# Attention projections of a hybrid backbone block: neighbouring channels exchanged by two transfers per head instead of a matrix product

## The chip, the cores and the metric

The kernel runs on one NeuronCore of a Trainium2 chip. The metric is the device time of one execution in microseconds (us). A core has five instruction queues that work side by side and meet only at semaphores: TensorE (PE in the rows; its weight loads are PEld), VectorE (DVE), ScalarE (ACT), GpSimd (POOL) and SyncE (SP), which issues the DMA transfers here.

## The reference

Two layers over 256 context tokens and 512 latent tokens of width 1024: an RWKV-7 layer, then a grouped-query attention layer, each followed by a SwiGLU feed-forward. The change is in the attention layer's projections. Cut to what matters:

```python
q = rms_norm((h @ wq).reshape(B, n, 8, 128), gq)      # 8 query heads
k = rms_norm((h @ wk).reshape(B, n, 2, 128), gk)      # 2 key heads
v = (h @ wv).reshape(B, n, 2, 128)
# rotation, latent tokens only, over pairs of neighbouring channels
x1, x2 = x[..., 0::2], x[..., 1::2]
out = stack([x1 * cos - x2 * sin, x1 * sin + x2 * cos])
```

Channels lie on the 128 partitions, tokens along the free axis. So `x * cos + partner(x) * sin` is wanted, where `partner` exchanges the partitions 2i and 2i+1, and the table `sin` carries the sign.

## The kernel before

The function `qkv` (lines 3001 on) makes v for all tokens, then ten heads one after the other: heads 0 and 1 are keys (768 tokens), heads 2 to 9 queries (512 latent tokens). Each engine runs a list of steps n = 0 to 11, and three heads are in work at once in a step:

- **Weights.** SP loads head n's weights, 512 KB, into one of two buffers `qk_w_raw` (`w.load`, L531). ACT rounds them (`w.round`, L536), POOL makes the remainder (`w.subtract`, L541). SP waits before load n only for the remainder of head n-2, which frees the buffer (L3058 to L3060).
- **PE, step n.** The product of head n: 24 matmuls with 512 columns (L561, called at L3084; for key heads 24 more with 256). Then the sum of squares of head n-1 by a product with ones (L3093). Then, for head n-2, the exchange of neighbouring channels: a product of the head in `qk_raw` with a permutation `swap` into bank 4 (L3103, two calls for two halves of the partitions, four instructions each in fp32 as the trace counts them for both together). It waits for `normed`.
- **ACT, step n.** First round the weights of head n+1 (L3125), then the square root for head n-1 (L3130), then copy head n from its bank to `qk_raw` (L3138) and square it (L3141). The copy of head n waits until head n-2 is `rotated`, since both use the same `qk_raw` buffer.
- **DVE, step n.** For head n-2: multiply by cos (L3168), wait for `swapped`, multiply the exchanged channels by sin (L3177), add (L3178, signals `rotated`). Then for head n-1: the reciprocal of the root (L3183), and the scaling (L3185), which signals `normed`.

Every engine's list is in program order, so an instruction whose semaphore is late holds all behind it on its engine. When all ten heads are done, a barrier ends the block and `attend` begins (it issues its own weight loads and starts with the scores).

Of the kernel before, what the change touches and what calls it, by code (L numbers as in the profile page):

```python
# [21 lines left out]
ALU = mybir.AluOpType  # L22
# [3 lines left out]
P = 128  # L26
D = 1024
CT = D // P
CTX, LAT = 256, 512
TOK = CTX + LAT  # L30
# [15 lines left out]
HEADS, KV_HEADS = 8, 2  # L46
# [35 lines left out]
def signal(eng, ins, sem, value):  # L82

    ins.then_inc(sem, 1)
    eng.wait_ge(sem, value)


def need(eng, sem, n):

    if not isinstance(n, int) or n > 0:  # L90
        eng.wait_ge(sem, n)
# [11 lines left out]
def half(h):  # L103

    return slice(CH * h, CH * h + CH)


class Core:
# [5 lines left out]
    def sb(self, name, shape):  # L114
        return self.ctx.enter_context(self.nc.sbuf_tensor(name, shape, F32))

    def sem(self, name):
        return self.ctx.enter_context(self.nc.semaphore(name))
# [439 lines left out]
def three_passes(pe, out, w, x, first, last, onto=False):  # L558

    for n, (a, b) in enumerate(((w[0], x[0]), (w[0], x[1]), (w[1], x[0]))):  # L560
        mm = pe.matmul(out, a, b, start=(first and n == 0), stop=(last and n == 2), skip_group_check=onto)  # L561
    return mm
# [2438 lines left out]
def qkv(c, d, h, hi, lo, q, k, v, norm):  # L3001
# [6 lines left out]
    NH = KV_HEADS + HEADS  # L3008
    KVD = KV_HEADS * P
    with ExitStack() as ctx:  # L3010
        sb = lambda n, s: ctx.enter_context(nc.sbuf_tensor(n, s, F32))
        sem = lambda n: ctx.enter_context(nc.semaphore(n))
        w = SplitWeights(c, ctx, "qk_w", CT, NH, (NH // 2, NH // 2))
        V_BANKS = (0, 1, 2, 3, 6, 7)
        wv = sb("wv", [P, CT, KVD])
        wv_hi, wv_lo = (ctx.enter_context(nc.sbuf_tensor(n, [P, CT, KVD], F32R)) for n in ("wv_hi", "wv_lo"))
        cos, sin, swap = sb("cos", [P, LAT]), sb("sin", [P, LAT]), sb("swap", [P, P])
        raw = [sb(f"qk_raw{s}", [P, TOK]) for s in range(2)]
        sq = [sb(f"qk_sq{s}", [P, TOK]) for s in range(2)]
        std, turned = sb("qk_std", [P, TOK]), sb("qk_turned", [P, LAT])  # L3020
# [1 line left out]
        tables, v_loaded, v_rounded = sem("rope_loaded"), sem("wv_loaded"), sem("wv_rounded")  # L3022
        v_rest = [sem(f"wv_rest{n}") for n in range(2)]
        v_product, v_copied = sem("v_product"), sem("v_copied")
        copied, squared, summed, rooted, normed, swapped, rotated, order_sem = (sem(n) for n in (
            "qk_copied", "qk_squared", "qk_summed", "qk_rooted", "qk_normed", "qk_swapped", "qk_rotated", "qk_dve_order"))
        wk = d["at_wk"][0].rearrange("(k p) e -> p k e", p=P)
        wq = d["at_wq"][0].rearrange("(k p) e -> p k e", p=P)

        def segs_of(n):  # L3030
            return SEGS if isinstance(n, int) and n < KV_HEADS else SEGS[1:]

        def steps(eng, step, order=None):

            for n in range(4):
                step(n, n % 2)
            for n in range(4, NH - 2):
                step(n, n % 2)
            for n in range(NH - 2, NH + 2):
                step(n, n % 2)  # L3040
# [5 lines left out]
        def there(n):  # L3046

            return not isinstance(n, int) or 0 <= n < NH

        with nc.Block() as block:  # L3050
            @block.sync
            def _(sp):
                sp.dma_start(wv[:], d["at_wv"][0].rearrange("(k p) e -> p k e", p=P)).then_inc(v_loaded, 16)
                for s in range(2):
                    w.load(sp, s, s, wk[:, :, s * P:(s + 1) * P])
                for t, s in ((cos, "k_cos"), (sin, "k_sin"), (swap, "k_swap")):
                    sp.dma_start(t[:], d[s]).then_inc(tables, 16)
                with sp.Fori(0, HEADS // 2) as i:  # L3058
                    for s in range(2):
                        w.load(sp, 2 * i + s + KV_HEADS, s, wq[:, :, bass.ds((2 * i + s) * P, P)])  # L3060

            @block.tensor
            def _(pe):
                norm.sums(pe)
                norm.spread(pe)
                for kt in range(CT):
                    norm.ready(pe, kt)
                    if kt % (CT // 2) == 0:
                        pe.wait_ge(v_rest[kt // (CT // 2)], 1)
                    for t in range(TOK // P):  # L3070
                        at = slice(t * P, t * P + P)
                        mm = three_passes(pe, c.bank[V_BANKS[t]][:, 0:KVD], (hi[:, kt, at], lo[:, kt, at]),
                                          (wv_hi[:, kt, :], wv_lo[:, kt, :]), kt == 0, kt == CT - 1)
                        if kt == CT - 1:
                            mm.then_inc(v_product, 1)
                pe.wait_ge(v_copied, TOK // P)

                def step(n, s, i=None):
                    if there(n):
                        pe.wait_ge(w.rest, w.at + n + 1)  # L3080
                        need(pe, copied, n - 1)
                        for kt in range(CT):
                            for at, width in segs_of(n):
                                mm = three_passes(pe, c.bank[2 * s + (at > 0)][:, 0:width], (w.hi[s][:, kt, :], w.lo[s][:, kt, :]),  # L3084
                                                  (hi[:, kt, at:at + width], lo[:, kt, at:at + width]),
                                                  kt == 0, kt == CT - 1)
                        mm.then_inc(w.product, 1)
                    if there(n - 1):

                        pe.wait_ge(squared, n)  # L3090
                        need(pe, rooted, n - 1)
                        for at, width in segs_of(n - 1):
                            mm = pe.matmul(c.bank[5 + (at > 0)][:, 0:width], c.ones[:], sq[1 - s][:, at:at + width],  # L3093
                                           start=True, stop=True)
                        mm.then_inc(summed, 1)
                    if there(n - 2):

                        if isinstance(n, int) and n == KV_HEADS:
                            pe.wait_ge(tables, 48)
                        pe.wait_ge(normed, n - 1)  # L3100
                        need(pe, rotated, n - 2)
                        for b in range(2):
                            mm = pe.matmul(c.bank[4][half(b), 0:LAT], swap[half(b), half(b)], raw[s][half(b), CTX:TOK],  # L3103
                                           start=True, stop=True)
                        mm.then_inc(swapped, 1)

                steps(pe, step)

            @block.scalar
# [49 lines left out]
            @block.vector  # L3159
            def _(dve):  # L3160
                order = Order(dve, order_sem)
                v_ = nc.vector

                def step(n, s, i=None):
                    if there(n - 2):
                        head = n - 2
                        x = raw[s]
                        order(v_.tensor_tensor(turned[:], x[:, CTX:TOK], cos[:], ALU.mult))  # L3168
                        dve.wait_ge(swapped, n - 1)
                        if isinstance(n, int) and head < KV_HEADS:  # L3170
                            o = k[:, head, CTX:TOK]
                            order(v_.tensor_copy(k[:, head, 0:CTX], x[:, 0:CTX]))
                        else:
                            at = head - KV_HEADS
                            at = slice(at, at + 1) if isinstance(n, int) else bass.ds(at, 1)
                            o = q[:, at, :].rearrange("p o t -> p (o t)")
                        order(v_.tensor_tensor(o, c.bank[4][:, 0:LAT], sin[:], ALU.mult))  # L3177
                        signal(dve, v_.tensor_tensor(o, o, turned[:], ALU.add), rotated, n - 1)  # L3178
                    if there(n - 1):
                        at = segs_of(n - 1)[0][0]  # L3180
                        gain = PGK if at == 0 else PGQ
                        dve.wait_ge(rooted, n)
                        order(v_.reciprocal(std[:, at:], std[:, at:]))  # L3183
                        x = raw[1 - s]
                        signal(dve, v_.scalar_tensor_tensor(x[:, at:], x[:, at:], c.par[:, gain:gain + 1], std[:, at:],  # L3185
                                                            ALU.mult, ALU.mult), normed, n)

                norm.invert(dve)
                norm.scale(dve, 0)
                norm.scale(dve, 1)  # L3190
                for k_tile in range(CT):
                    if k_tile + 2 < CT:
                        norm.scale(dve, k_tile + 2)
                    norm.low(dve, k_tile)
                steps(dve, step, order)


# [284 lines left out]
```

## Time and profile before

| | |
|---|---|
| median of 3 runs | 2188.77 us (2188.66 to 2190.41) |
| profiled execution, span | 2190.7 us |
| attention projections with their norm and v | about 1497 to 1632.5 us of that span |
| the ten heads, from the first scaling's start to the last sum's end | 1556.3 to 1632.4 us |
| PE busy over the span | 92% |
| DVE, ACT, POOL busy | 55%, 38%, 17% |

The span is what the profiler saw from the first to the last instruction of one execution; it is 1.9 us over the median of the runs. Times in rows are counted from the start of that span.

### The profile page before, as it was taken

To read this page: it belongs to the slowest core of one execution; us is meant where nothing else is said; L and a number is where in the kernel's file an instruction comes from. 1 tells how busy PE (TensorE), PEld (TensorE's weight loads), DVE (VectorE), ACT (ScalarE), POOL (GpSimd) and SP (SyncE) were. 2 spreads that over 40 slices of the span, in tenths; PEclk is the share of its full clock that TensorE was granted. 3 is DMA by queue.
4 is the path that set the end of the run, shared out by engine and by line. 5 is a ranking of instruction groups with operands and counts; after the bars stand their busy time and mean duration, and the time that the engine had idled before them with its cause. 6 is when DMAs were issued, how large, how long until landed. Compare 5 with 4: busy or idle time off the path is not lost. (4 is left out here: it accounts for less than half of the span.)

```text
span 2190.7 us, 52634 instructions
## 1 busy us (share of the span) xinstructions
PE 2022.6 (92%) x22455; PEld 1755.4 (80%) x22455; DVE 1209.5 (55%) x1909; ACT 830.5 (38%) x1395; POOL 365.9 (17%) x387
## 2 busy tenths in 40 slices
PE   5799997899999988689999999998979988999998
PEld 3688885688888887689999999998645577888887
DVE  4865435566666663328857667565675534333333
ACT  2433324455555533226324233234325424422321
POOL 0000001566666652020000000002210010000000
PEclk8799998799999999789999999998989998999999
DMA  9577774001111000511212122112110013332332
GB/s 317 178 238 228 230 239 140 19 19 30 34 35 36 18 12 11 180 59 40 94 58 77 59 80 75 58 58 59 58 29 1 1 58 96 96 112 81 97 112 78
DMA packets 223496, 191.70 MB, mean 88 GB/s; under 512 B 12970, under 2 KB 208180, under 8 KB 222772
## 3 DMA queue, kind: packets, MB, share of 16 engines
q1 hardware_dynamic: 223284, 188.58, 27.8%
q8 instruction: 169, 2.77, 0.5%
q14 instruction: 43, 0.35, 0.1%
HBM read 170.73 MB, written 17.83 MB: 86 GB/s over the span
## 5 line engine op out<-in xcount | busy, mean ns | idle before, releaser
L541 DVE TENSOR_TENSOR ffn_lo<-ffn_raw,ffn_hi 128x1024 fp32r<-128x1024 f32 (+1 forms) x58 | 77.5, 1335 | 196.5 <-ACT ffn_hi L536 196.5
L561 PE MATMUL banks<-operand_hi,ffn_w_hi 128*128 128x384 f32 x464 | 155.9, 336 | 4.4 <-DVE operand_lo L507 4.4
L561 PE MATMUL banks<-operand_lo,ffn_w_hi 128*128 128x384 f32 x464 | 155.6, 335 | 0.0
L561 PE MATMUL banks<-operand_hi,ffn_w_lo 128*128 128x384 f32 x464 | 155.5, 335 | 0.0
L561 PE MATMUL banks<-mix_hi,proj_hi 128*128 128x386 f32 (+1 forms) x384 | 136.6, 356 | 14.8 <-DVE proj_lo L733 9.5
L561 PE MATMUL banks<-operand_hi,ffn_hi 128*128 128x512 f32 x352 | 138.6, 394 | 5.2 <-DVE operand_lo L507 2.8
L561 PE MATMUL banks<-operand_hi,ffn_lo 128*128 128x512 f32 x352 | 138.1, 392 | 0.0
L561 PE MATMUL banks<-operand_lo,ffn_hi 128*128 128x512 f32 x352 | 138.1, 392 | 0.0
L536 ACT CAST ffn_hi<-ffn_raw 128x1024 fp32r<-128x1024 f32 (+1 forms) x60 | 68.3, 1139 | 183.2 <-PE banks L561 182.4
L561 PE MATMUL banks<-mix_hi,proj_lo 128*128 128x386 f32 (+1 forms) x384 | 131.8, 343 | 0.0
L561 PE MATMUL banks<-mix_lo,proj_hi 128*128 128x386 f32 (+1 forms) x384 | 131.8, 343 | 0.0
L431 POOL TENSOR_TENSOR norm_squares<-norm_squares,norm_x 128x768 f32<-128x768 f32 (+1 forms) x18 | 29.8, 1654 | 588.3 <-ACT norm_x L425 588.3
L2827 ACT CAST ffn_w_hi<-ffn_raw 128x512 fp32r<-128x512 f32 (+1 forms) x116 | 68.7, 605 | 130.2 <-PE banks L561 130.1
L2060 POOL TENSOR_TENSOR lvl<-sc_b,level_mask 128x256 f32<-128x256 f32 x144 | 109.6, 777 | 48.1 <-DVE sc_b L1792 34.2
L561 PE MATMUL banks<-ffn_t_hi,ffn_w_hi 128*128 128x384 f32 x320 | 106.9, 334 | 0.0
L561 PE MATMUL banks<-ffn_t_lo,ffn_w_hi 128*128 128x384 f32 x320 | 106.9, 334 | 0.0
L561 PE MATMUL banks<-ffn_t_hi,ffn_w_lo 128*128 128x384 f32 x320 | 106.9, 334 | 0.0
L2994 DVE SCALAR_TENSOR_TENSOR residual_stream<-banks,mod,residual_stream 128x256 f32<-128x256 f32 x144 | 60.8, 478 | 73.4 <-PE banks L561 73.2
L561 PEld LDWEIGHTS banks<-mix_hi,proj_hi 128*128 128x128 f32 x384 | 73.9, 192 | 30.4 <-issue 15.3
L2898 DVE TENSOR_TENSOR ffn_w_lo<-ffn_raw,ffn_w_hi 128x512 fp32r<-128x512 f32 (+1 forms) x112 | 77.5, 693 | 26.6 <-ACT ffn_w_hi L2827 25.0
L1808 DVE TENSOR_TENSOR inverse<-banks,inverse 128x256 f32<-128x256 f32 x120 | 50.7, 423 | 73.8 <-PE banks L1578 72.6
L561 PEld LDWEIGHTS banks<-operand_hi,ffn_w_hi 128*128 128x128 f32 x464 | 87.6, 189 | 4.7 <-DVE operand_lo L507 4.7
(320 smaller groups left out, 5714.0 us busy)
## 6 DMA issues: line engine op xcount, KB each, us to landing
mod_raw<-in_mod_w SPq DMA_DIRECT2D x96, 512.0 KB, 5.1
ffn_raw<-in_ff_w SPq DMA_DIRECT2D x32, 1024.0 KB, 5.3
ffn_raw<-in_ff_w SPq DMA_DIRECT2D x46, 512.0 KB, 3.8
ffn_raw<-in_ff_w SPq DMA_DIRECT2D x16, 704.0 KB, 4.6
proj_raw<-in_rw_wr SPq DMA_DIRECT2D x16, 256.0 KB, 5.1
proj_raw<-in_rw_wk SPq DMA_DIRECT2D x16, 256.0 KB, 6.1
proj_raw<-in_rw_wv SPq DMA_DIRECT2D x16, 256.0 KB, 6.0
rwkv_out_raw<-in_rw_wo SPq DMA_DIRECT2D x8, 512.0 KB, 4.4
```

Of the source, the lines that this page charges most:

```text
L431: pool.tensor_tensor(self.pool_sum[:, self.at0:], self.pool_sum[:, self.at0:], self.x[:, s, self.at0:], ALU.add)\
L536: signal(act, self.nc.scalar.copy(self.hi[s][:, 0:k_tiles, :], self.raw[s][:, 0:k_tiles, :]), self.rounded, self.at + n + 1)
L541: signal(eng, eng.tensor_tensor(self.lo[s][:, 0:k_tiles, :], self.raw[s][:, 0:k_tiles, :], self.hi[s][:, 0:k_tiles, :].bitcast(F32), ALU.s ...
L561: mm = pe.matmul(out, a, b, start=(first and n == 0), stop=(last and n == 2), skip_group_check=onto)
L1808: v.tensor_tensor(x, by_way(work(self.use, "y", G.g, n), n), x, ALU.add).then_inc(x_added, 1)
L2060: g.tensor_tensor(flat(lvl[G.parity][n % 2][:]).rearrange("p (a b x) -> p a b x", **blocks), lower_blocks(sc_b[G.third][:], n), flat(level ...
L2827: nc.scalar.copy(w_hi[x.n % SLOTS][:, 0:x.k_tiles, :], source(x)).then_inc(rounded, 1)
L2898: v.tensor_tensor(w_lo[x.n % SLOTS][:, k, :], source(x), w_hi[x.n % SLOTS][:, k, :].bitcast(F32), ALU.subtract)\
L2994: v.scalar_tensor_tensor(h[:, m, at:at + width], c.bank[bank_no(self, "down", part, m, q)][:, col:col + width], c.mod[:, 0, 40 + m, r:r + ...
```

## The change

`swap` and its table load go. A buffer `qk_partner` (128 partitions by 512 tokens) is added in SBUF. For each head SP now issues two transfers from SBUF to SBUF: one takes the even partitions of `qk_raw` to the odd ones of `qk_partner`, the other the odd to the even. SP's loop over the query weights becomes a plain list of steps: load the weights of head n, wait until head n-2 is normed and head n-3 rotated, issue the two transfers of head n-2. DVE waits for these transfers (32 per head) where it waited for PE, and multiplies `partner` by sin instead of bank 4. DVE waits for the tables, which PE did before. PE's exchange, with its waits, is gone.

```diff
-        cos, sin, swap = sb("cos", [P, LAT]), sb("sin", [P, LAT]), sb("swap", [P, P])
+        cos, sin, partner = sb("cos", [P, LAT]), sb("sin", [P, LAT]), sb("qk_partner", [P, LAT])
...
-                for t, s in ((cos, "k_cos"), (sin, "k_sin"), (swap, "k_swap")):
+                for t, s in ((cos, "k_cos"), (sin, "k_sin")):
                     sp.dma_start(t[:], d[s]).then_inc(tables, 16)
-                with sp.Fori(0, HEADS // 2) as i:
-                    for s in range(2):
-                        w.load(sp, 2 * i + s + KV_HEADS, s, wq[:, :, bass.ds((2 * i + s) * P, P)])
+                for n in range(2, NH + 2):
+                    if n < NH:
+                        at = (n - KV_HEADS) * P
+                        w.load(sp, n, n % 2, wq[:, :, at:at + P])
+                    sp.wait_ge(normed, n - 1)
+                    need(sp, rotated, n - 2)
+                    for b in range(2):
+                        sp.dma_start(partner[1 - b:P:2, :], raw[n % 2][b:P:2, CTX:TOK]).then_inc(swapped, 16)
...
-                    if there(n - 2):
-
-                        if isinstance(n, int) and n == KV_HEADS:
-                            pe.wait_ge(tables, 48)
-                        pe.wait_ge(normed, n - 1)
-                        need(pe, rotated, n - 2)
-                        for b in range(2):
-                            mm = pe.matmul(c.bank[4][half(b), 0:LAT], swap[half(b), half(b)], raw[s][half(b), CTX:TOK],
-                                           start=True, stop=True)
-                        mm.then_inc(swapped, 1)
...
+                        if n == KV_HEADS:
+                            dve.wait_ge(tables, 32)
                         order(v_.tensor_tensor(turned[:], x[:, CTX:TOK], cos[:], ALU.mult))
-                        dve.wait_ge(swapped, n - 1)
+                        dve.wait_ge(swapped, 32 * (n - 1))
...
-                        order(v_.tensor_tensor(o, c.bank[4][:, 0:LAT], sin[:], ALU.mult))
+                        order(v_.tensor_tensor(o, partner[:], sin[:], ALU.mult))
```

## Rows read from the trace of the kernel before

**Rows 1.** The page's first line.
```profile
span 2190.7 us, 52634 instructions
```

**Rows 2.** Busy time by stretch: columns PE, PEld, DVE, ACT, POOL, then clock and DMA.
```profile
1576.00:1608.00 32.00, 30.41 (x121) 19.97 (x121) 29.36 (x21) 11.39 (x16) 9.52 (x4) 1.00 0.16 47
```

**Rows 3.** DVE in order of time: head 0's scaling, then one whole query step.
```profile
1556.26 1.02 DVE L3185 SCALAR_TENSOR_TENSOR qk_raw<-qk_raw,par,qk_std 128x768 f32<-128x768 f32 x1
...
1574.74 0.69 DVE L3168 TENSOR_TENSOR qk_turned<-qk_raw,cos 128x512 f32<-128x512 f32 x1
1575.95 0.69 DVE L3177 TENSOR_TENSOR q_heads<-banks,sin 128x512 f32<-128x512 f32 x1 [0.52 <-PE banks L3103]
1576.68 0.69 DVE L3178 TENSOR_TENSOR q_heads<-q_heads,qk_turned 128x512 f32<-128x512 f32 x1
1577.41 3.35 DVE L3183 RECIPROCAL qk_std<-qk_std 128x512 f32<-128x512 f32 x1
1580.80 1.91 DVE L3185 SCALAR_TENSOR_TENSOR qk_raw<-qk_raw,par,qk_std 128x512 f32<-128x512 f32 x1
```

**Rows 4.** DVE: head 1, then the scalings of heads 6 to 9, then the last sum.
```profile
1560.38 4.95 DVE L3183 RECIPROCAL qk_std<-qk_std 128x768 f32<-128x768 f32 x1
1565.37 1.02 DVE L3185 SCALAR_TENSOR_TENSOR qk_raw<-qk_raw,par,qk_std 128x768 f32<-128x768 f32 x1
...
1604.82 1.92 DVE L3185 SCALAR_TENSOR_TENSOR qk_raw<-qk_raw,par,qk_std 128x512 f32<-128x512 f32 x1
...
1612.82 0.75 DVE L3185 SCALAR_TENSOR_TENSOR qk_raw<-qk_raw,par,qk_std 128x512 f32<-128x512 f32 x1
...
1620.38 0.75 DVE L3185 SCALAR_TENSOR_TENSOR qk_raw<-qk_raw,par,qk_std 128x512 f32<-128x512 f32 x1
...
1628.12 0.75 DVE L3185 SCALAR_TENSOR_TENSOR qk_raw<-qk_raw,par,qk_std 128x512 f32<-128x512 f32 x1
...
1631.74 0.69 DVE L3178 TENSOR_TENSOR q_heads<-q_heads,qk_turned 128x512 f32<-128x512 f32 x1
```

**Rows 5.** ACT in order of time: head 1's root, then one rounding and one root.
```profile
1557.39 1.05 ACT L3130 ACTIVATE qk_std<-banks,eps 128x256 f32<-128x256 f32 x2 [3.59 <-DVE qk_raw L3185]
...
1578.61 1.03 ACT L536 CAST qk_w_hi<-qk_w_raw 128x1024 fp32r<-128x1024 f32 x1
1582.82 0.69 ACT L3130 ACTIVATE qk_std<-banks,eps 128x512 f32<-128x512 f32 x1 [3.18 <-DVE qk_raw L3185]
```

**Rows 6.** POOL in order of time: one remainder of a head's weights.
```profile
1579.78 2.38 POOL L541 TENSOR_TENSOR qk_w_lo<-qk_w_raw,qk_w_hi 128x1024 fp32r<-128x1024 f32 x1 [5.62 <-ACT qk_w_hi L536]
```

**Rows 7.** PE in order of time: a product's first matmul, the sums, the exchange.
```profile
1575.77 0.50 PE L561 MATMUL banks<-operand_hi,qk_w_hi 128*128 128x512 f32 x1
...
1581.35 1.02 PE L3093 MATMUL banks<-qk_sq,ones 128*128 128x512 f32 x2
1582.76 1.08 PE L3103 MATMUL banks<-qk_raw,swap 64*64 64x512 f32 x4 [0.39 <-DVE qk_raw L3185]
```

**Rows 8.** SP: one weight load's issue, and the landing times of all eight.
```profile
1582.33 0.38 SPq L531 DMA_DIRECT2D qk_w_raw<-in_at_wq  x1
```
```profile
DMA to landing us min/median/max: 3.8/4.0/4.3
```

**Rows 9.** Other transfers: count, KB each, median us from issue to landing.
```profile
out<-y_rows SPq DMA_DIRECT2D x4, 512.0 KB, 2.8
...
v_all<-shifted SPq DMA_DIRECT2D x1, 384.0 KB, 2.3
...
ident<-in_k_ident SPq DMA_DIRECT2D x1, 64.0 KB, 1.9
```

**Rows 10.** Stretches at the lower clock (columns as in rows 2), and PE's sums there.
```profile
1512.00:1515.00 3.00, 3.00 (x14) 3.00 (x15) 2.84 (x6) 1.36 (x3) 0.00 (x0) 0.50 0.00 0
```
```profile
1618.00:1621.00 3.00, 2.08 (x2) 0.50 (x2) 2.96 (x2) 0.28 (x1) 0.00 (x0) 0.50 0.00 0
```
```profile
1618.33 2.08 PE L3093 MATMUL banks<-qk_sq,ones 128*128 128x512 f32 x2 [2.91 <-ACT qk_sq L3141]
```

## The prediction

> **What bounds the stage now.** The change touches only the ten heads of the attention projections, so I left the page after its first line, the span of 2190.7 us [rows 1], and read the stage in this order: busy time by stretch, then each engine's timeline. By stretch, PE is busy 30.4 of 32 us and DVE 29.4 [rows 2]; the share doesn't say who leads. DVE's timeline does. One query step there is: cos product 0.69, a wait of 0.52 for PE's exchange, sin product 0.69, sum 0.69, reciprocal 3.35, scaling 1.91, with some 0.04 between instructions [rows 3]. That makes 8.0 us, and DVE waits for nothing in it but the exchange. PE needs 5.58 us for a product (1575.77 to 1581.35), 1.0 for the sums and 1.1 for the exchange [rows 7], and waits for DVE's `normed`. So DVE leads, by a loop from `normed` to `normed`. I write N0 to N9 for the ends of the ten scalings: N0 = 1556.26 + 1.02 = 1557.28 [rows 3]; N1 = 1566.39, N6 = 1606.74, N7 = 1613.57, N8 = 1621.13, N9 = 1628.87, and the last sum ends at 1632.43 [rows 4]. The gaps: N0 to N1 9.11, N1 to N6 40.35 (five gaps), then 6.83, 7.56, 7.74, and 3.56 at the end.
>
> **What is removed.** PE loses 1.08 us per head. PE doesn't lead, so that alone is worth nothing. DVE loses its 0.52 us wait for PE, if what takes its place is no longer than the cos product.
>
> **What is added on DVE's side.** Two transfers stand between `normed` and the sin product. SP issues an instruction 0.17 us after the engine it waits for has ended (POOL ends at 1579.78 + 2.38 = 1582.16 [rows 6], the issue starts at 1582.33 [rows 8]), and an issue takes 0.38 [rows 8], 0.4 with the gap. No row shows a transfer from SBUF to SBUF. The nearest: 64 KB into SBUF 1.9 us, 384 KB out of SBUF 2.3, 512 KB out of SBUF 2.8 [rows 9]. For 128 KB out of and into SBUF I take 2.3, between 1.9 and 2.8; a gain is excluded, as each is far above the 0.69 of the cos product. So `partner` is there at 0.17 + 0.4 + 2.3 = 2.9 us after `normed`, and DVE waits some 2.2 us where it waited 0.52.
>
> The Trainium skill, in "DMA: Bandwidth & Descriptors", section "Anatomy of one DMA", fits a fixed 2.0 us plus the bytes at 436 GB/s for transfers issued by GpSimd; as an estimate that is 2.3 us for 128 KB, and no row here shows this kind of transfer.
>
> **What is moved: the weight loads.** This is the larger part. Before, load n+1 waits only for the remainder of head n-1, long done when its weights are needed. Now it stands in SP's list behind the two transfers of head n-2, thus behind N(n-2). And round n+1 is the first thing in ACT's step n, ahead of the root for head n-1 (L3125, L3130). So the root of head n-1, and with it N(n-1), waits for a load that is issued only after N(n-2). That closes a new loop, from `normed` through SP, the load, ACT and DVE back to `normed`:
>
> - SP's reaction 0.17, two issues 0.8;
> - the load, from issue to landing: 3.8 to 4.3, median 4.0 [rows 8]; I take 4.2, since 256 KB of exchange go just ahead of it on the same queue. Bounds 3.8 and 4.8;
> - rounding 1.03 and root 0.69 [rows 5], reciprocal 3.35 [rows 3];
> - scaling 0.75, not 1.91. It is 0.75 where POOL does nothing (heads 7 to 9 [rows 4]) and 1.9 where POOL's remainder runs beside it (1580.80 lies in 1579.78 to 1582.16 [rows 3, 6]). In the new loop POOL works from 6.4 to 8.8 us after `normed` and the scaling starts at 10.4, so it is clear of it. This is a real gain, 1.15 us a head, inside the loss;
> - four hand-overs of 0.04.
>
> Sum: 0.17 + 0.8 + 4.2 + 1.03 + 0.69 + 3.35 + 0.75 + 0.16 = 11.15 us a head, for 8.0. The exchange (ready at 2.9, DVE done with the rotation at 4.3) is hidden in it: the reciprocal can't start before 6.9. Cover left: 2.6 us.
>
> PE in this loop: the remainder ends at 8.76 us (load 5.17, rounding to 6.24, then 0.14 and 2.38); product and sums take 5.58 + 1.02 = 6.6 [rows 7] and end at 15.4. The root that needs them can't start before the next round has ended, at 11.15 + 6.25 = 17.4. So PE has 2 us to spare, at the full clock.
>
> **The sum.** Loads 3 to 9 gate N1 to N7.
> N0 to N1: as above, but root 1.05 [rows 5], reciprocal 4.95 and scaling 1.02 [rows 4]: 13.4, against 9.11: +4.3.
> N1 to N6: 5 x 11.15 = 55.75, against 40.35: +15.4.
> N6 to N7: 11.15 against 6.83: +4.3.
> N7 to N8: no load is ahead of this root. It waits for the sums, at 15.4 us after N6, so it ends 5.0 after N7; with reciprocal and scaling 9.2, against 7.56: +1.6.
> N8 to N9: exchange 2.9, sin, sum, reciprocal, scaling: 8.5, against 7.74: +0.8.
> The end: 2.9 + 0.69 + 0.69 + 0.08 = 4.3, against 3.56: +0.8.
> Together +27.2 us. The first load and N0 don't move; the DVE's wait for the tables is met 45 us before; nothing after the block depends on when it ends, so the shift passes to the end in full. On the profiled execution: 2190.7 + 27.2 = 2217.9; on the median 2188.77: 2216.0.
>
> **Rivals.**
> 1. *PE at the lower clock.* In the new loop PE idles some 4.5 us of 11.15. In the trace an idle stretch of 2.9 us is followed by sums at a granted clock of 0.50, the 1.2 GHz level, which take 2.08 us for 1.02 [rows 7, 10]. A product at that level from end to end would take twice its time: the remainder at 8.76, then 13.2, then root, reciprocal, scaling and hand-overs 4.9, makes 26.9 us over two heads, 13.4 each: 2.3 more for seven heads, +43 in all, 2232. Against it: when dense products begin after the idle stretch at 1512, the clock stays at 0.50 for 3 us [rows 10] and is full later; three such microseconds cost 1.5 to 1.6 and fit into PE's 2 us. 0.20 that the clock costs over 3 us in all.
> The Trainium skill, "TensorE: Matmul & The Clock Gate", section "HAM oscillation", says the same of kernels whose PE waits for a load between bursts: every burst begins throttled. By that rule each product starts at 1.2 GHz; the trace agrees at the 0.50 of rows 10, but not on what it would cost here.
> 2. *Transfers that are slow or block SP.* Every second partition as source and target is a pattern that no row shows. If the load lands 2 us later for it, seven heads pay 14 more: 2230. 0.07.
> 3. *Only the latency counts.* If the loads' place doesn't bind (they land early or ACT is not held), DVE pays the exchange alone: 2.9 + 1.45 + 3.35 + 0.75 to 1.9 + 0.1 = 8.5 to 9.7 a head, +5 to +17: 2194 to 2206. Against it: the order in the lists of SP and ACT. 0.08.
> 4. *Faster.* DVE without any wait and its scaling clear of POOL would need 0.69 x 3 + 3.35 + 0.75 + 0.2 = 6.3 us a head, 1.7 less: -13, 2176. It decides where the exchange is there within 0.7 us of `normed` and the load's chain to the root within 2.2; the shortest landing in the rows is 1.9 [rows 9]. 0.03.
> 5. *No effect*, the two costs and gains in balance: 0.02.
>
> **How the numbers follow.** The forecast case has 0.60: 2216, by the bounds of the load (3.8 to 4.8, -2.8 to +4.2) and of the issues 2211 to 2221. The range takes in rivals 1 and 2: 2210 to 2232. A measurement of this kernel tells some 0.2% (4 us) from no change; slower by more holds 0.60 + 0.20 + 0.07 + 0.08 = 0.95, within it 0.02, faster 0.03.
>
> **What would show it.** After: DVE's scalings 11 us apart for heads 2 to 7 and 8.5 to 9 for the last two; scaling 0.75 throughout; before ACT's rounding an idle stretch whose releaser is the DMA of `qk_w_raw`; weight loads issued about 1 us after each scaling ends, at even distance, not in time with POOL's remainder; DVE's long wait at the reciprocal for ACT, not at the sin product. The prediction is wrong if DVE's long wait is at the sin product (rival 3 or slow exchanges), or if ACT's root waits for PE (rival 1).

## The result, and the profile after

The changed kernel takes 2225.02 us (median of 4 runs, 2223.91 to 2227.69), the kernel before on the same chip 2189.59 (4 runs, 2188.66 to 2192.96). The ratio is 1.0158, with a 95% interval of 1.0145 to 1.0171: slower by 34.6 us, 31.8 to 37.4. The forecast was 2216.0, with 2210 to 2232 as its range. In the profiled execution the span grew from 2190.7 [rows 1] to 2222.6.

```profile
span 2222.6 us, 52540 instructions
```

The stage tells where. N0, the end of head 0's scaling, is 1557.49 (1557.28 before), and the last sum ends at 1663.97 + 0.69 = 1664.66 (1632.43 before [rows 4]). From N0 to there the stage takes 107.17 us instead of 75.15: +32.0, while the span grew by 31.9. So the loss lies in this stage, to within 0.3 us.

DVE in order of time, from the scaling of head 2 to that of head 3; then the scalings of heads 4, 6, 7, 8, 9 and the last sum (start, duration, and in brackets the idle time before it with its releaser):

```profile
1581.89 0.75 DVE L3182 SCALAR_TENSOR_TENSOR qk_raw<-qk_raw,par,qk_std 128x512 f32<-128x512 f32 x1
1582.68 0.69 DVE L3165 TENSOR_TENSOR qk_turned<-qk_raw,cos 128x512 f32<-128x512 f32 x1
1585.40 0.69 DVE L3174 TENSOR_TENSOR q_heads<-qk_partner,sin 128x512 f32<-128x512 f32 x1 [2.03 <-DMA qk_partner<-qk_raw]
1586.13 0.69 DVE L3175 TENSOR_TENSOR q_heads<-q_heads,qk_turned 128x512 f32<-128x512 f32 x1
1590.66 3.35 DVE L3180 RECIPROCAL qk_std<-qk_std 128x512 f32<-128x512 f32 x1 [3.85 <-ACT qk_std L3125]
1594.05 0.75 DVE L3182 SCALAR_TENSOR_TENSOR qk_raw<-qk_raw,par,qk_std 128x512 f32<-128x512 f32 x1
...
1605.93 0.75 DVE L3182 SCALAR_TENSOR_TENSOR qk_raw<-qk_raw,par,qk_std 128x512 f32<-128x512 f32 x1
...
1629.62 0.75 DVE L3182 SCALAR_TENSOR_TENSOR qk_raw<-qk_raw,par,qk_std 128x512 f32<-128x512 f32 x1
...
1640.72 0.75 DVE L3182 SCALAR_TENSOR_TENSOR qk_raw<-qk_raw,par,qk_std 128x512 f32<-128x512 f32 x1
...
1651.48 0.75 DVE L3182 SCALAR_TENSOR_TENSOR qk_raw<-qk_raw,par,qk_std 128x512 f32<-128x512 f32 x1
...
1659.78 0.75 DVE L3182 SCALAR_TENSOR_TENSOR qk_raw<-qk_raw,par,qk_std 128x512 f32<-128x512 f32 x1
...
1663.97 0.69 DVE L3175 TENSOR_TENSOR q_heads<-q_heads,qk_turned 128x512 f32<-128x512 f32 x1
```

Against [rows 3] two idle stretches are new. One of 2.03 us, ahead of the sin product, is the transfer's latency. The other, 3.85 us ahead of the reciprocal, has nothing to do with the exchange: it waits for ACT's root. Beside them stands a gain: the scaling takes 0.75 in every step, and no longer 1.91. Why ACT is late stands in SP's and ACT's lists. SP in order of time (SPq is its issuing), the two transfers of head 2 and the load behind them:

```profile
1582.67 1.11 SPq L3065 DMA_DIRECT2D qk_partner<-qk_raw  x2
1583.82 0.59 SPq L531 DMA_DIRECT2D qk_w_raw<-in_at_wq  x1
```

ACT in order of time, the rounding that this load feeds, the root behind it, and two later roots:

```profile
1588.80 1.04 ACT L536 CAST qk_w_hi<-qk_w_raw 128x1024 fp32r<-128x1024 f32 x1 [9.26 <-DMA qk_w_raw<-in_at_wq]
1589.88 0.69 ACT L3125 ACTIVATE qk_std<-banks,eps 128x512 f32<-128x512 f32 x1
...
1601.76 0.69 ACT L3125 ACTIVATE qk_std<-banks,eps 128x512 f32<-128x512 f32 x1 [0.40 <-PE banks L3098]
...
1647.31 0.69 ACT L3125 ACTIVATE qk_std<-banks,eps 128x512 f32<-128x512 f32 x1 [8.94 <-PE banks L3098]
```

This is the loop. The scaling ends at 1582.64, SP issues at 1582.67 to 1583.78, then the load from 1583.82; it lands and ACT rounds at 1588.80, takes the root at 1589.88, and DVE may invert at 1590.66. ACT had been ready for 9.26 us when the load landed. The root starts right after the rounding. The sums that it reads were not much earlier, though: PE in order of time,

```profile
1587.79 1.02 PE L3098 MATMUL banks<-qk_sq,ones 128*128 128x512 f32 x2
```

They end at 1588.81, so ACT's list holds this root for some 1.0 us only; the product ahead of them had waited for the load before. That matters in experiment 3. The waits summed over the stage (window 1536 to 1670; us in total, times, longest):

```profile
ACT qk_w_hi L536 <- DMA qk_w_raw<-in_at_wq: 63.7, 7, 10.5
...
DVE qk_std L3180 <- ACT qk_std L3125: 49.7, 9, 24.1
...
DVE q_heads L3174 <- DMA qk_partner<-qk_raw: 16.1, 8, 2.1
```

The 49.7 holds 24.1 of the wait before the first head, which belongs to the stage's start.

### The profile page after: what moved, and what is told of

It is laid out like the page before. It is cut to its first block and busy times, and to the rows that moved or that the text cites. A ratio compares the mean times of both kernels' runs of the same rounds, so it can differ in the third digit from the quotient of the medians.

```text
span 2222.6 us, 52540 instructions
## 1 busy us (share of the span) xinstructions
PE 2025.8 (91%) x22415; PEld 1766.3 (79%) x22415; DVE 1203.3 (54%) x1909; ACT 830.3 (37%) x1395; POOL 365.3 (16%) x387
## 5 line engine op out<-in xcount | busy, mean ns | idle before, releaser
L2898 DVE TENSOR_TENSOR ffn_w_lo<-ffn_raw,ffn_w_hi 128x512 fp32r<-128x512 f32 (+1 forms) x112 | 77.5, 693 | 27.2 <-ACT ffn_w_hi L2827 25.6
```

The lines of the kernel that those rows point to most:

```text
L2898: v.tensor_tensor(w_lo[x.n % SLOTS][:, k, :], source(x), w_hi[x.n % SLOTS][:, k, :].bitcast(F32), ALU.subtract)\
```

## The experiments

Nine kernels. The theory is that of the prediction: the loads' place closes a loop through SP, ACT and DVE. Against it stand the latency of the transfers alone, and the lower clock of PE, as the cause of what the sum missed. "Stage" is N0 to the end of the last sum: 75.15 us before, 107.17 after. It compares profiles better than their spans do, since N0 lies between 1552 and 1562 us in them; from the issue of v's weights to N0 they all take 60.0 to 60.1 us, but for experiment 4 (63.7). Each ratio is to runs of the kernel before on the same chip, beside the experiment: median 2194.53 us for 1 to 4, 2189.80 for 5 to 7.

**1. The loads taken out of the loop.** SP issues load n+1 ahead of its wait for head n-2; the transfers stay.

```diff
-                for n in range(2, NH + 2):
+                def load(n):
                     if n < NH:
                         at = (n - KV_HEADS) * P
                         w.load(sp, n, n % 2, wq[:, :, at:at + P])
+
+                load(2)
+                for n in range(2, NH + 2):
+                    load(n + 1)
                     sp.wait_ge(normed, n - 1)
                     need(sp, rotated, n - 2)
```

> The changed kernel, with the weight load of head n+1 issued ahead of SP's wait for head n-2 instead of behind it. Theory A (the loss comes from weight loads queued behind the transfers' wait): the loop through the load opens, and DVE pays only the transfers: 0.7 cos, 2.0 wait, 0.7 + 0.7, reciprocal 3.35, scaling 0.75 to 1.9 (POOL's remainder moves back beside it) makes 8.4 to 9.6 us a head instead of 11.7; total 2200 to 2207 us. Theory B (the loss is the transfers' own latency and PE's clock): the loads don't matter, 11.5 us a head and 2222 to 2226 us remain.

Measured: 2205.48 us (2204.43 to 2209.08), ratio 1.0062 [1.0041, 1.0084]; stage 87.50, heads 9.45 to 9.79 us apart while POOL works and 8.30 afterwards, as theory A expected. ACT waits for no load. DVE in order of time:

```profile
1590.69 0.69 DVE L3178 TENSOR_TENSOR q_heads<-qk_partner,sin 128x512 f32<-128x512 f32 x1 [2.02 <-DMA qk_partner<-qk_raw]
...
1592.14 3.35 DVE L3184 RECIPROCAL qk_std<-qk_std 128x512 f32<-128x512 f32 x1
1595.53 1.87 DVE L3186 SCALAR_TENSOR_TENSOR qk_raw<-qk_raw,par,qk_std 128x512 f32<-128x512 f32 x1
```

The wait at the reciprocal is gone, that of 2.02 at the sin product remains, and the scaling is back at 1.87, beside POOL's remainder (1594.51 to 1596.85). So the change costs two things: 87.50 - 75.15 = 12.35 us for the latency of the exchange (DVE waits 20.4 us for it over ten heads, where it waited 7.8 for PE's), and 107.17 - 87.50 = 19.7 for the place of the loads on top of it. The split holds in this order; the two overlap in the changed kernel, so they don't simply add. This kernel is what rival 3 of the prediction described (8.5 to 9.7 a head, +5 to +17).

**2. The place of the loads alone.** The kernel before, with PE's exchange and no transfer from SBUF to SBUF, but each query load n waits for `normed` of head n-3, as in the changed kernel.

```diff
-                with sp.Fori(0, HEADS // 2) as i:
-                    for s in range(2):
-                        w.load(sp, 2 * i + s + KV_HEADS, s, wq[:, :, bass.ds((2 * i + s) * P, P)])
+                for n in range(2, NH):
+                    at = (n - KV_HEADS) * P
+                    need(sp, normed, n - 2)
+                    w.load(sp, n, n % 2, wq[:, :, at:at + P])
```

> The kernel before, with PE's product for the exchange, no transfer at all, but each query weight load held until the head three before it is normed, as in the changed kernel. Theory A: the loop through the load is there without any transfer: reaction 0.1, load 4.3, rounding 1.0, root 0.7, reciprocal 3.35, scaling 0.75, hand-overs 0.2 makes 10.4 us a head, and 2205 to 2213 us in all, 16 to 24 over before. Theory B: no transfer, no loss: 2189 us, heads 8.0 us apart.

Measured: 2226.68 us (2215.35 to 2228.92), ratio 1.0141 [1.0105, 1.0177]; stage 110.1; the heads are 10.1 to 13.5 apart up to N8. That the loads' place alone makes the kernel slower is shown. The size was missed, and the waits of the stage say why (us in total, times, longest):

```profile
ACT qk_w_hi L536 <- DMA qk_w_raw<-in_at_wq: 56.1, 7, 9.1
...
DVE q_heads L3178 <- PE banks L3104: 27.1, 8, 7.1
```

The second line is the new one: the exchange of head n-2 is in PE's list behind the product of head n, and a product that waits for late weights holds it. So a second loop closes, through PE, which the changed kernel hasn't, since its exchange doesn't pass PE. The 31 us here, where 16 to 24 were expected, are therefore no measure of the loads' part in the change; experiment 1 is.

**3. The root ahead of the rounding.** The changed kernel, two blocks of ACT's step swapped, to cut the loop at ACT.

```diff
-                    if not isinstance(n, int) or n + 1 < NH:
-                        w.round(act, n + 1, 1 - s, pair_of(n, s, i), CT)
                     if there(n - 1):
                         act.wait_ge(summed, n)
...
                         ins.then_inc(rooted, 1)
+                    if not isinstance(n, int) or n + 1 < NH:
+                        w.round(act, n + 1, 1 - s, pair_of(n, s, i), CT)
```

> The changed kernel, but in ACT's step the root of head n-1 stands ahead of the rounding of head n+1's weights. Theory A: the root no longer waits for the load, but PE's product still does: the loop now spans two heads, load 5.5, rounding 1.0, POOL 2.5, product and sums 6.6 to 8.2 by the clock, root to scaling 4.9, so 10.3 to 11.1 us a head instead of 11.7: 2215 to 2221 us. If ACT's order has no part in it: 2225 us.

Measured: 2237.3 us (2236.18 to 2239.54), ratio 1.0203 [1.0183, 1.0224]; heads 13.5 to 13.7 apart. All expectations missed. ACT in order of time:

```profile
1591.69 0.69 ACT L3123 ACTIVATE qk_std<-banks,eps 128x512 f32<-128x512 f32 x1 [10.59 <-PE banks L3098]
1592.28 1.03 ACT L536 CAST qk_w_hi<-qk_w_raw 128x1024 fp32r<-128x1024 f32 x1
```

The root now waits 10.59 us for PE's sums, which stand behind the product of head n, and the rounding for head n+1 stands behind the root. So PE's product, the root, the rounding, the remainder and the next product run one after another. The load has landed by then (no wait for it is left). The edit made a third loop and therefore says nothing on the one it was meant to cut.

**4. What the clock costs.** The changed kernel with 16 extra products after each step's sums, into a bank that nobody reads any more: extra work, to keep PE busy while it waits.

```diff
                         mm.then_inc(summed, 1)
+                    if n < NH - 1:
+                        for _ in range(16):
+                            pe.matmul(c.bank[4][:, 0:LAT], wv_hi[:, 0, 0:P], hi[:, 0, CTX:TOK], start=True, stop=True)
```

> The changed kernel with 16 extra products of 512 columns into the unused bank 4 after the sums of each of the first nine steps, some 3.6 us, so that PE idles less between the heads' products. Their result is read by nobody. Theory A with the clock as the second term: the products run at the higher clock from end to end (5.6 instead of some 7 us), the root never waits for the sums, and the gap from the eighth to the ninth scaling falls from 10.8 to 9.3 us: 2220 to 2223 us. If the clock has no part: 2225 us. If the extra products delay the next one they cost up to 1 us a head.

Measured: 2224.09 us (2221.89 to 2227.07), ratio 1.0146 [1.0126, 1.0167]. Busy time by stretch (columns as in rows 2), first of the changed kernel,

```profile
1592.00:1604.00 12.00, 9.39 (x27) 6.86 (x27) 6.30 (x6) 2.84 (x4) 2.67 (x2) 0.74 0.21 66
```

then of this one:

```profile
1604.00:1628.00 24.00, 21.52 (x88) 16.42 (x89) 13.29 (x11) 5.69 (x8) 4.75 (x2) 1.00 0.22 66
```

The granted clock rises from 0.74 to 1.00, and the stage shrinks from 107.17 to 103.82. Of these 3.35 us, N7 to N8 holds 1.54 (10.76 to 9.22, the 9.2 of the prediction), and two roots that waited for the sums, by 0.40 and 0.62, no longer do. These 2.6 us are the clock's. The rest is the path from `normed` to the rounding, which took 5.41 us a step and not 5.66; nothing shows that the clock has a part in that.

The run times (2225.0 and 2224.1, ranges that overlap) don't show the gain, and the edit itself explains it: the extra products also run ahead of N0, where the root waits for them. ACT in order of time:

```profile
1551.44 1.05 ACT L3128 ACTIVATE qk_std<-banks,eps 128x256 f32<-128x256 f32 x2 [10.65 <-PE banks L3098]
```

That wait is 7.02 in the changed kernel. The 3.6 us lost there take back the 3.35 won in the stage.

**5 to 7. Can the latency be hidden?** Experiment 1 left 2.0 us of wait ahead of the sin product, and the reciprocal of head n-1 right behind it, which doesn't need the exchange. So the reciprocal goes ahead of the wait, and `qk_raw` gets a third buffer, so that ACT's copy of head n waits until head n-3 is `rotated`, and no longer for head n-2. The core of the edit:

```diff
-        raw = [sb(f"qk_raw{s}", [P, TOK]) for s in range(2)]
+        raw = [sb(f"qk_raw{s}", [P, TOK]) for s in range(3)]
...
-                        need(act, rotated, n - 1)
+                        need(act, rotated, n - 2)
...
                         order(v_.tensor_tensor(turned[:], x[:, CTX:TOK], cos[:], ALU.mult))
+                        if there(n - 1):
+                            invert(n)
                         dve.wait_ge(swapped, 32 * (n - 1))
```

5 is experiment 1 with both edits, 6 the kernel before with both (PE's exchange), 7 experiment 1 with the third buffer alone.

> The changed kernel with three edits: loads first (as in the run of that name), a third buffer for the head being normed so that ACT's copy of head n waits for head n-3 and not n-2 to be rotated, and DVE's reciprocal for head n-1 moved between the cos product and the wait for the transfers. Theory A (once the loads are free, only the transfers' latency on DVE is left): the 3.35 us reciprocal covers the 2.0 us wait; DVE needs 0.69 x 3 + 3.35 + 0.75 + 0.2 = 6.4 us a head and PE 5.5 + 1.0 = 6.5, so 6.5 to 7 us a head, less than the 8.0 of before: 2179 to 2185 us. If something else of the transfers costs time, it stays over 2190.

> The kernel before, with PE's product for the exchange, and the same third buffer and moved reciprocal, so that what the order is worth without any transfer can be told from what the transfers are worth. Theory A: DVE's wait of 0.52 and the collision with POOL go, but PE must do product 5.5, sums 1.0 and exchange 1.1, so 7.6 to 7.9 us a head: 1 to 4 us under before, 2186 to 2189 us, and slower than the kernel that has both the order and the transfers. If the transfers bring nothing of their own, the two are equal.

> The changed kernel with loads first and the third buffer, but DVE's order as in the changed kernel. POOL's remainder moves ahead of the scaling, so the scaling takes 0.75 us and not 1.9; the transfers are still waited for: 0.69, 2.0, 1.4, 3.35, 0.75 and 0.2 makes 8.4 us a head against 9.46 in the run with loads first alone. Total 2196 to 2201 us; if the scaling's 1.9 us has another cause than POOL, it stays near 2205.

Measured: 5, 2194.66 us (2190.55 to 2197.4, 12 runs), ratio 1.0014 [1.0001, 1.0027], stage 78.40. 6, 2188.08 us (12 runs), ratio 0.9990 [0.9975, 1.0004], stage 71.14: the time was expected, but not that it would be faster than 5. 7, 2202.89 us (6 runs), ratio 1.0050 [1.0034, 1.0066], stage 87.09. So 5 takes back most of the loss, but it and 7 missed what was expected. The waits of 5's stage:

```profile
ACT qk_w_hi L536 <- DMA qk_w_raw<-in_at_wq: 16.8, 5, 3.7
ACT qk_std L3129 <- PE banks L3102: 13.1, 2, 7.0
...
DVE q_heads L3185 <- DMA qk_partner<-qk_raw: 2.0, 1, 2.0
```

The exchange is hidden (2.0 us over all heads, where it was 16.1), but the loads are late again. Load n+1 is ahead of the wait for head n-2, yet still behind the one for head n-3, one step earlier in SP's list. The shorter the step, the sooner that binds: gaps of 6.5 to 6.8 us between heads take turns with some of 10.6 and 13.3. DVE products that meet POOL take up to 2.83 us for 0.69 in it as well. In 7 the rounding waits for its load too (20.1 us over six heads), so POOL's remainder comes too late to clear the scaling, which stays at 1.52 to 2.09.

**8 and 9. The exchange issued by another engine.** Now SP issues loads alone, as before the change, and ACT issues the two transfers after its root; third buffer and moved reciprocal stay.

```diff
                         ins.then_inc(rooted, 1)
+                    if there(n - 2):
+                        act.wait_ge(normed, n - 1)
+                        need(act, rotated, n - 2)
+                        for b in range(2):
+                            act.dma_start(partner[1 - b:P:2, :], raw[(n - 2) % 3][b:P:2, CTX:TOK]).then_inc(swapped, 16)
```

> As the run with loads first, third buffer and moved reciprocal, but the two transfers are issued by ACT, right after the root of head n-1, and SP is left with the weight loads alone, each issued as soon as its buffer is free, as in the kernel before. Theory A (in that run loads still stood behind transfers in SP's list, now of the head before, and ACT waited 17 us for them): ACT waits for no load, the transfers land some 4 us after the scaling ends, still under the reciprocal, and the heads come 6.5 to 7 us apart: 2179 to 2185 us, 4 to 10 under before. If the transfers bring nothing even then, or ACT's 1.1 us of issuing holds the loop: 2188 us or more.

Measured: 2189.65 us (12 runs), before 2190.02, ratio 1.0000 [0.9990, 1.0011]; stage 74.12. No wait for a load is left, but the heads are 8.17 apart while POOL works and 6.48 afterwards, so the 2179 to 2185 of theory A was missed. DVE in order of time, and POOL:

```profile
1585.22 2.36 DVE L3181 TENSOR_TENSOR q_heads<-qk_partner,sin 128x512 f32<-128x512 f32 x1
```

```profile
1584.69 2.34 POOL L541 TENSOR_TENSOR qk_w_lo<-qk_w_raw,qk_w_hi 128x1024 fp32r<-128x1024 f32 x1 [5.83 <-ACT qk_w_hi L536]
```

The sin product takes 2.36 beside POOL, where it takes 0.69 alone: 1.67 more, which is the difference of 8.17 and 6.48. [rows 3] has no sin product beside POOL, but experiment 6 has, with the operand still in a PSUM bank. DVE and POOL there:

```profile
1583.82 0.69 DVE L3184 TENSOR_TENSOR q_heads<-banks,sin 128x512 f32<-128x512 f32 x1
1584.54 0.96 DVE L3185 TENSOR_TENSOR q_heads<-q_heads,qk_turned 128x512 f32<-128x512 f32 x1
```

```profile
1582.55 2.40 POOL L541 TENSOR_TENSOR qk_w_lo<-qk_w_raw,qk_w_hi 128x1024 fp32r<-128x1024 f32 x1 [5.70 <-ACT qk_w_hi L536]
```

The sin product lies wholly beside POOL and keeps its 0.69; the sum behind it, with both operands in SBUF, takes 0.96. Experiment 9 moves POOL's work: ACT rounds head n+2's weights right after the root and the issue, one step sooner.

```diff
+                w.round(act, 1, 1, 0, CT)
                 def step(n, s, i=None):
-                    if not isinstance(n, int) or n + 1 < NH:
-                        w.round(act, n + 1, 1 - s, pair_of(n, s, i), CT)
...
+                    if n + 2 < NH:
+                        w.round(act, n + 2, s, (n + 2) // 2, CT)
```

> As the run in which ACT issues the transfers, but ACT rounds the weights of head n+2 right after the root of head n-1 and the issue, ahead of the copy and the square, and so one step sooner. In that run POOL's remainder (2.34 us) lay beside the sin product, which took 2.36 us where it had been 0.69 with its operand in PSUM. Theory C (a DVE instruction with two operands in SBUF waits for POOL, one with an operand in PSUM or with a single operand doesn't): POOL now starts 2.5 us after the scaling ends, beside the reciprocal, which reads one operand; the sin product falls to 0.7 to 1.3, and the heads come 6.5 to 7.2 us apart instead of 8.17: 2182 to 2186 us. If the 2.36 us come from the transfers themselves, they stay, and the total with them: 2188 to 2190.

Measured: 2185.9 us (2180.32 to 2192.53, 12 runs), before 2191.39 (17 runs), ratio 0.9974 [0.9960, 0.9988]; stage 68.29, heads 7.02 apart. DVE in order of time:

```profile
1576.64 3.35 DVE L3164 RECIPROCAL qk_std<-qk_std 128x512 f32<-128x512 f32 x1 [0.16 <-ACT qk_std L3120]
1580.02 1.24 DVE L3183 TENSOR_TENSOR q_heads<-qk_partner,sin 128x512 f32<-128x512 f32 x1
```

and POOL beside it:

```profile
1578.34 2.38 POOL L541 TENSOR_TENSOR qk_w_lo<-qk_w_raw,qk_w_hi 128x1024 fp32r<-128x1024 f32 x1 [4.65 <-ACT qk_w_hi L536]
```

POOL ends at 1580.72, 0.70 after the sin product has begun, and it takes 0.55 longer than 0.69. So the collision moves with POOL's place, as theory C expected (0.7 to 1.3, heads 6.5 to 7.2 apart). This version beats both kernels, the one before by 5.5 us (2.6 to 8.8). That it owes this to the transfers isn't shown: it and experiment 6, which keeps PE's product, have intervals that overlap (0.9960 to 0.9988 and 0.9975 to 1.0004), though its stage is 2.9 us shorter.

## Why the prediction was right, step by step

The mechanism was right and the sign with it; the sum was too small by 4.8 us on the profiled stage. The terms, in us:

| | before | predicted | after |
|---|---|---|---|
| N0 to N1 | 9.11 | 13.4 | 13.63 |
| N1 to N6 | 40.35 | 55.75 | 59.25 |
| N6 to N7 | 6.83 | 11.15 | 11.10 |
| N7 to N8 | 7.56 | 9.2 | 10.76 |
| N8 to N9 | 7.74 | 8.5 | 8.30 |
| N9 to the end | 3.56 | 4.3 | 4.13 |
| sum | 75.15 | 102.3 | 107.17 |

- **DVE leads, and the place of the loads is the larger part.** Shown by experiment 1: 19.7 of 32.0 us go when the loads leave the loop. Of the signs that were named, these are there: ACT idle ahead of the rounding with the load as releaser, DVE's long wait at the reciprocal for ACT, the load issued 1.17 to 1.23 us after a scaling. The scalings of heads 2 to 7 are 11.1 to 12.2 apart where 11 was said, and the last two gaps are 10.76 and 8.30 where 8.5 to 9 was said. One sign of being wrong, ACT's root waiting for PE, shows in two steps between N1 and N6 and between N7 and N8; the point on the clock has its price.
- **The path from `normed` to the rounding** was put at 5.17 (0.17 + 0.8 + 4.2). Five steps measure 5.52, 6.16, 5.51, 5.63 and 5.46, mean 5.66. SP's reaction was too long in the sum (0.03 measured, not 0.17) and the issues too short: a transfer from SBUF to SBUF takes 0.55 to issue, not 0.38, so the pair takes 1.15 with the gap behind it, not 0.8. The load then takes 4.3 to 5.0 from issue to rounding, mean 4.48 where 4.2 was taken; one of the five is over the upper bound of 4.8. Together that is 0.49 a step, 2.4 of the 3.5 us missing in N1 to N6. The kind of transfer was in no row, and the sum names no bounds for the issues.
- **The clock** was the rival that came half true. PE was given 2 us to spare, and a product at the lower clock for its first 3 us was to take 1.5 of them. PE in order of time, the first matmul of the product of head 5 and the sums behind it:

```profile
1592.38 0.80 PE L561 MATMUL banks<-operand_hi,qk_w_hi 128*128 128x512 f32 x1 [3.57 <-POOL qk_w_lo L541]
...
1600.65 1.02 PE L3098 MATMUL banks<-qk_sq,ones 128*128 128x512 f32 x2
```

  From its first matmul to the sums the product takes 8.27 us, where 5.58 was taken from [rows 7]; 13 of its 24 matmuls are 0.43 apart, twice the distance of the others. The six products from 1580 to 1646 measure 7.56, 8.27, 7.22, 8.44, 7.21 and 7.20. The two over 8 are 2.7 and 2.9 longer than at full clock, more than the 2 us to spare, and so their roots wait, 0.40 above (1601.76) and 0.62 in the other case. N7 to N8, which waits for the sums with nothing to spare, loses 1.5. The step "the clock stays at 0.50 for 3 us" failed: in the product above the wide spacing lasts 5.7 us. With it failed the claim that it fits into the 2 us. The rival's own size failed as well (the whole product at the lower clock, 13.4 a head, 2232): the clock is worth 2.6 us by experiment 4, not 16. The Trainium skill, "TensorE: Matmul & The Clock Gate", section "HAM oscillation", says that bursts between waits for a load begin throttled. The trace agrees in part: over such a step the granted clock is 0.74, and the four products after 3.45 to 5.12 us of idle time are slow from their first matmul. The two after 2.01 and 2.23 us begin with matmuls 0.23 to 0.24 apart and turn slow after five and seven of them.
- **The exchange's latency** was right: landing 1.9 to 2.1 (2.3 was taken), the longer issue makes it up, and `partner` is there 2.76 us after `normed` (2.9 predicted). DVE waits 2.03 (2.2 predicted). It is hidden in the loop of the loads, as was said: it costs its full 12.35 us only once the loads are free (experiment 1).
- **The gain in the scaling** was right: 0.75 in every step from head 2 on, since POOL's remainder (from 1589.99) comes well ahead of it. It lay in the 11.15, and experiment 1 loses it again with the loop. The rival "faster" fails at both its conditions: the landing is 1.9, and the load's chain to the root takes 7.2 us (1582.64 to 1589.88), not 2.2.

The interval of the runs, +31.8 to +37.4, holds the profile's 32.0. It is above the 27.2 of the sum, and 2225 is also above the forecast's own bounds of 2211 to 2221. What is missing is the longer path (2.4) and rival 1 at a small part of its price (1.0 in N1 to N6 and 1.6 in N7 to N8). The stated range covers it only because it took in the rivals.

## What to carry to other kernels

A step that is moved to a queue brings its waits along: ask what stands behind the wait in that list. Here prefetches did, and that cost more (19.7 us) than the latency of the transfers (12.35); an engine that issues prefetches should wait for nothing late. In these runs transfers in place of a product drew level only once the consumer had independent work to put ahead of the wait (the reciprocal, 3.35 us) and no load stood behind them, and came out ahead only with less of POOL beside the operand that moved from PSUM to SBUF.

## What the runs showed of the hardware

- **A DVE product pays for where its operand lies, if POOL runs.** With the exchanged operand in a PSUM bank the sin product took 0.69 wholly beside POOL's remainder (experiment 6); in SBUF it took 2.36 where it began beside the remainder and 1.24 where it overlapped it by 0.70 us. In each of four cases the DVE instruction ends 0.54 to 0.55 us after POOL's: the sin product at 1587.58 after 1587.03 (experiment 8) and at 1581.26 after 1580.72 (9), the scaling at 1597.40 after 1596.85 (1) and at 1582.71 after 1582.16 [rows 3, 6]. So it looks as if it did its work only when POOL had finished. The Trainium skill, "SBUF — State Buffer", section "SBUF: two separate sides", says that VectorE with two SBUF inputs and a GpSimd instruction that reads SBUF lock each other out of one port for a whole instruction. The four ends agree.

  A single operand is no safe rule. The reciprocal kept its 3.35 in the changed kernel, though it began beside the remainder (1590.66, with POOL from 1589.99 to 1592.33). But a copy from SBUF to SBUF, 0.29 alone, took 2.24 in experiment 8, beside POOL from 1568.00 to 1570.34:

```profile
1568.25 2.24 DVE L3176 COPY k_heads<-qk_raw 128x256 f32<-128x256 f32 x1
```

  In the changed kernel nothing of this costs time, as its loop keeps all but the reciprocal clear of POOL.
- **Transfers from SBUF to SBUF** over every second partition, 128 KB each: the tile's own view in the changed kernel, count with issue times in ns (min, median, max), and landing.

```profile
L3065 SPq DMA_DIRECT2D qk_partner<-qk_raw x20: 465/554/599, 1557.5 to 1661.1; - x20
```

```profile
DMA to landing us min/median/max: 1.9/2.0/2.1
```

  They land in 2.0, where a plain 64 KB into SBUF takes 1.9 [rows 9]; what pattern, source and size each do to that no run separates. The issue takes 0.55, where a weight load's took 0.38 [rows 8], and that of the load behind the pair takes 0.59.
